# B turned between products, a bank of its own for the first modulation columns, the third scan inside a selection, and split query turns

## Time and profile before

| | us |
|---|---|
| median of three runs | 1421.62 |
| the three runs | 1420.0, 1421.62, 1423.72 |
| the profiled execution, its own time | 1424.93 |
| its span | 1422.8 |
| PE busy in it | 1379.6 (97%) |
| DVE busy in it | 800.9 (56%) |
| ACT busy in it | 351.1 (25%) |
| POOL busy in it | 261.1 (18%) |

### The profile page before, as it was taken

One profiled execution on the slowest core, in us unless ns is written; L12 is line 12 of the kernel. 1 busy time (PEld: TensorE's weight loads), 2 busy tenths in 40 slices (PEclk: granted clock), 3 DMA queues, 4 the chain that ended last, 5 costly groups with the idle time before them and its releaser, 6 DMA issues.

```text
span 1422.8 us, 16091 instructions
## 1 busy us (share of the span) xinstructions
PE 1379.6 (97%) x5860; PEld 860.6 (60%) x5860; DVE 800.9 (56%) x1915; ACT 351.1 (25%) x859; POOL 261.1 (18%) x261
## 2 busy tenths in 40 slices
PE   3999998999999999999999999999999999999999
PEld 2544555545544545555455566444578888888887
DVE  5777899538441453113555667112557676777363
ACT  4123221115300102111455567010022323230000
POOL 1167466305002386500000000000000000000000
PEclk9999998999999999999999999999999999999999
DMA  9672323542403112200301001030323131314120
GB/s 342 177 167 75 99 38 88 155 164 89 149 0 108 59 60 85 93 30 16 133 1 60 1 1 49 19 112 0 104 72 106 61 117 60 119 60 159 60 71 30
DMA packets 85769, 120.58 MB, mean 85 GB/s; under 512 B 15256, under 2 KB 43230, under 8 KB 85692
## 3 DMA queue, kind: packets, MB, share of 16 engines
q1 hardware_dynamic: 80992, 110.80, 24.5%
q10 hardware_dynamic: 2956, 5.05, 1.1%
q0 software_dynamic: 1744, 3.70, 1.0%
HBM read 111.00 MB, written 6.84 MB: 83 GB/s over the span
## 4 chain that ended last, share of the span: by engine, by line
PE 95%; DVE 3%; issue 1%; ACT 1%; DMA 0%; ACTq 0%; DVEq 0%
PE bank L776 24%; PE bank L1311 17%; PE bank L1337 9%; PE bank L788 8%; PE bank L1222 6%; PE bank L808 5%; PE bank L1063 4%; PE bank L1178 3%; PE bank L1202 3%; PE bank L838 2%; PE bank L1281 2%; PE bank L1075 2%; PE bank L1391 1%; PE bank L1031 1%; PE bank L1160 1%
## 5 line engine op out<-in xcount | busy, mean ns | idle before, releaser
L776 PE MATMUL bank<-arena 128*128 128x512 f32 (+1 forms) x800 | 343.9, 587 | 1.4 <-ACT arena L1659 1.0
L776 PEld LDWEIGHTS bank<-arena 128*128 128x128 f32 x800 | 151.4, 192 | 174.5 <-issue 169.4
L1311 PE MATMUL bank<-arena 128*128 128x256 f32 x1120 | 242.0, 379 | 0.0
L1311 PEld LDWEIGHTS bank<-arena 128*128 128x128 f32 x1120 | 212.7, 190 | 29.7 <-issue 0.8
L808 PEld LDWEIGHTS bank<-arena 128*128 128x128 f32 (+2 forms) x692 | 85.4, 147 | 69.2 <-issue 47.9
L1337 PE MATMUL bank<-arena 128*128 128x256 f32 x560 | 122.5, 380 | 0.0
L1337 PEld LDWEIGHTS bank<-arena 128*128 128x128 f32 x560 | 105.9, 190 | 16.1 <-issue 1.7
L808 PE MATMUL bank<-arena 128*128 128x128 f32 (+2 forms) x692 | 99.8, 284 | 14.7 <-DMA arena<-in_a_im 3.5
L788 PE MATMUL bank<-arena 128*128 128x512 f32 x256 | 113.2, 596 | 0.0
L1836 POOL TENSOR_TENSOR arena<-arena 128x1 f32<-128x1 f32 x8 | 4.4, 553 | 479.5 <-DVE arena L2037 479.5
L2560 DVE CUSTOM_DVE_ANT_0 arena<-bank,arena 128x128 f32<-128x128 f32 (+3 forms) x128 | 57.7, 488 | 58.9 <-PE bank L1178 58.1
(11 more groups left out here) (345 smaller groups left out, 1732.5 us busy)
## 6 DMA issues: line engine op xcount, KB each, us to landing
arena<-in_w_in SPq DMA_DIRECT2D x14, 2048.0 KB, 7.9
arena<-in_w_up SPq DMA_DIRECT2D x20, 1024.0 KB, 6.9
arena<-in_w_ada SPq DMA_DIRECT2D x8, 1024.0 KB, 13.2
arena<-in_w_down SPq DMA_DIRECT2D x8, 1024.0 KB, 7.4
arena<-in_w_ada SPq DMA_DIRECT2D x2, 2048.0 KB, 8.5
arena<-in_w_out SPq DMA_DIRECT2D x2, 2048.0 KB, 7.8
arena<-in_w_attn_br SPq DMA_DIRECT2D x2, 2048.0 KB, 8.5
arena<-in_w_o SPq DMA_DIRECT2D x2, 2048.0 KB, 7.9
```

Of the source, the lines that this page charges most:

```text
L776: mm = pe.matmul(ps[:, 0:n], act[:, k, 128 * t:128 * t + 128], w[:, k, 0:n], start=(k == 0), stop=(k == kt - 1))
L1311: mm = pe.matmul(ps, left[:, k, :], right[:, k, :], start=(first and k == 0), stop=(k == 3), skip_group_check=True)
```

## The change

Five edits. The naming of banks:

```diff
-        name_aux("ccol", "lam", "cols", "rb", "rb2", ("mod", 0), *[("x", k) for k in range(KT)], ("mod", 1),
-                 ("mod", 2), ("mod", 3), "c1", "c2", "bt0", "bt1", "cols2")
+        name_aux("ccol", "lam", "cols", "rb", "rb2")
+        name_aux(("mod", 0), banks=3)
+        name_aux(*[("x", k) for k in range(KT)], ("mod", 1), ("mod", 2), ("mod", 3), "c1", "c2", "bt0", "bt1", "cols2")
```

The product u by single k, with B's turns between its products:

```diff
+            def u_part(k, j0=0, j1=4, bt=None):
...
+                if bt is not None:
+                    pb = begin_aux(f"bt{bt}")
+                for j in range(j0, j1):
+                    ps = begin_proj(("u", j)) if k == 0 else pbank(("u", j))
+                    mm = pe.matmul(ps[:, :], w[:, k, 128 * j:128 * j + 128], hT[:, k, :],
+                                   start=(k == 0), stop=(k == KT - 1))
...
+                    if bt is not None:
+                        for m in range(4 * j, 4 * j + 4):
+                            mm = pe.transpose(pb[:, 32 * m:32 * m + 32], braw[bt][0:32, m:2048:GC], ident[0:32, 0:32])
...
-            u_step(0, 0, 3)
+            for k in range(3):
+                u_part(k)
             mod_turn(2)
-            u_step(0, 3, 4)
+            u_part(3, 0, 2)
             mod_turn(3)
+            u_part(3, 2, 4)
...
+            u_part(4)
             pe.wait_ge(b_in, 64)
...
-            u_step(1, 4, 8)
+            u_part(5, bt=0)
+            u_part(6, bt=1)
+            u_part(7)
```

The query turns of block two, and the wait behind `ypm`:

```diff
             for m in range(4):
                 turn(("qt2", m), [row2[:, t, 128 * m:128 * m + 128] for t in range(TT)])
+            one_rows("m00", 0, "m00", hT)
             pe.wait_ge(qrope_done, 2 * TT)
             for m in range(4):
                 turn(("qt2", 4 + m), [q2b[:, t, 128 * m:128 * m + 128] for t in range(TT)])
-
-            for m in range(4, 8):
-                aux_out(pe, ("qt2", m))
-            one_rows("m00", 0, "m00", hT)
             one_rows("m00", 1, "m00", hT)
...
-            for j in range(4):
-                proj_out(pe, ("ypm", j))
-
             def fill2(name):
                 key, t = name
+                if name == ("yp0", 0):
+                    for j in range(4):
+                        proj_out(pe, ("ypm", j))
```

The third scan, on DVE:

```diff
-            topk(2, TOPK // 8, True)
+            topk(2, 8)
+            scan(2)
+            topk(2, TOPK // 8 - 8, True)
             gelu_in(0)
             gelu_in(1)
-            scan(2)
             topk(3, TOPK // 8, True)
```

More of the change, by code:

```diff
@@ L825, in x_turns @@
                     turn((key, k), [src[:, t, 128 * k:128 * k + 128] for t in range(TT)])
-            def u_step(s, k0, k1):
-                pe.wait_ge(wu_in[s], 16)
-                w = slot_view(0, KT, 512)
[L831 to L835, removed]
-                    for j in range(4):
[L837 to L841, removed]
+            def u_part(k, j0=0, j1=4, bt=None):
+                pe.wait_ge(wu_in[k // 4], 16)
+                if k % 2:
+                    pe.wait_ge(hv_ready, k // 2 + 1)
+                else:
+                    pe.wait_ge(ha_ready, k // 2 + 1)
+                w = slot_view(0, KT, 512)
+                if bt is not None:
[4 more added lines that the diff above has]
+                                   start=(k == 0), stop=(k == KT - 1))
+                    if k == KT - 1:
+                        mm.then_inc(proj_done, 1)
+                    if bt is not None:
+                        for m in range(4 * j, 4 * j + 4):
+                            mm = pe.transpose(pb[:, 32 * m:32 * m + 32], braw[bt][0:32, m:2048:GC], ident[0:32, 0:32])
+                if bt is not None:
+                    mm.then_inc(aux_done, 1)
             def mod_turn(s):
```

## The result

| | before | changed |
|---|---|---|
| median, us (9 runs each) | 1422.06 | 1414.97 |
| lowest to highest | 1420.0 to 1423.72 | 1410.71 to 1418.6 |
| the profiled execution: time, span | 1424.93, 1422.8 | 1411.54, 1409.3 |
| mean granted clock in it | 0.99 | 0.996 |

The ratio is 0.9949, with a 95% interval of 0.9933 to 0.9964: 7.1 us faster, where 6.7 had been forecast (1415). A second group of six runs of the same kernel gave 1414.78, ratio 0.9944 (0.9932 to 0.9957).

A forecast was written before the change was run, and what follows sets the result against it. PE, busy in 97% of the span, was taken as the bound, with gains in its waits and slowed stretches. Block one's -0.8 and block two's -5.9 us made -6.7, so 1415 us; eight in ten from 1404 to 1419.

The forecast's parts named there:

- the wait that it forecast: Before PE's turns of q in block one: a new wait of 8 to 12 us for the norm of q.
- a clock that falls elsewhere: Sign of being wrong: PE's clock falling in places other than those forecast; no size given.
- (a): Turns of x at the start: bank 3 removes PE's 2.90 us wait and the chain behind moves whole, -2.9 us.
- (b): u's second half: with B's turns between products the clock stays full, -3.2 us.
- (c): B's turns within u: each of 8 returns to a large product may cost 0.2 us, +0.8 (0 to 1.6).
- (d): After u: DVE waits for B's copy, POOL's tables start 1.4 us later, PE waits under 1 us, made up by idle time.
- the turns between products cost what they save: Rival, chance 0.13: B's turns within u lose 3.2 us, taken in by the wait at q's turns; 1417.5 to 1420.
- The third scan, and what it meets: Block one: scan 13.2 us earlier saves PE 8.9, but POOL's tables stretch gelu_in from 4.2 to 14 us; new wait equals gain.
- the port costs little: Rival, chance 0.22: POOL's operations don't take turns with gelu_in; block one gives -10 to -13, so 1402 to 1407.
- The clock behind that wait: After the wait at q's turns: fallen clock costs 1.7 us in 16 turns and 1.3 in the z product.
- Block one, net: At ssm_out(3): all edits of block one together bring PE there 0.8 us earlier.
- Block two: Row 0 of m00 between the query turns saves 4.8 us, the moved wait behind ypm 1.1: sum -5.9.

The follow-up runs named there:

- changed_again: The changed kernel itself, unaltered, measured once more in a later group: 1414.78 us, ratio 0.9944.
- b_block: The changed kernel with B's 32 small turns in one block again, ahead of u's second half: 1409.7 us, ratio 0.9914.
- bank_only: The kernel before with only bank 3 for the first modulation columns: 1418.88 us, ratio 0.9975.
- pool_held_b_block: The changed kernel with POOL's last tables held until gelu_in is done and B's turns in one block: 1403.41 us, ratio 0.9869.
- b_early: The changed kernel with B's turns between u's products of k = 4 and 5, not 5 and 6: 1411.64 us, ratio 0.9934.
- scan_only: The kernel before with only the third scan moved inside the second selection: 1424.43 us, ratio 1.0015.
- gelu_late: The changed kernel with gelu_in(0) and gelu_in(1) moved behind 12 rounds of topk(3): 1410.41 us, ratio 0.9921.
- pool_held: The changed kernel with POOL's tables of the last quarter held until gelu_in(0) and gelu_in(1) are done: 1408.71 us, ratio 0.9910.
- block2_only: The kernel before with only block two's split query turns and the moved wait behind ypm: 1419.31 us, ratio 0.9975.
- the start alone: The kernel before with only bank 3 for the first modulation columns and B's turns between products of u: 1421.47 us, ratio 0.9992.
- no_scan: The changed kernel with the third scan back behind gelu_in: 1415.76 us, ratio 0.9955.

## Why the prediction was right, and where its terms were off

The sum (-6.7) met the result (-7.1), and the wait that it forecast is there at its place and size. That the number came so close was luck in part. The terms as the profiles measure them give more: with `changed_again`, whose run of 1415.19 us is near its median, block one is 2.1 us shorter up to y(3), block two 6.0 and its compressed scores 1.7, together some 10 us in the span, and 3 of them are the slow draw of the profile of before. One of its own signs of being wrong, a clock that falls elsewhere, shows in `changed_again`: at u's first records, and in the compressed scores (0.97).

**The start, (a).** Right, and too small, since it said only that the chain moves whole. The 2.90 us went. Besides, with no pause in the turns of x the clock came up within them: 2.0 us in the turns, 0.8 in `mod_turn(1)` and 2.4 in u's first 24 records. PE was 8.9 us early at ki, not 5.3: 2.9 + 5.2, and 0.8 from B's turns. In `changed_again` it was 6.6: there u's first 24 records took 12.10 us, with a granted clock of 0.68 and 0.89 from 32 to 40 us. Another 2.1 may be the draw of the profile of before.

**(b) and (c), B's turns.** In u's second half, with its turns, the clock stayed full, as forecast, in every profile that has them. The price of the switches was mis-sized: forecast 0 to 1.6 us. (With it u's second half took 19.8 us, 49.40 to 69.23, where 17 to 19 were forecast.) A group of one product and four turns takes 1.61 us, eight of them 12.9; in `b_block` the 32 turns take 3.67 us (49.88 to 53.55), and eight products at full clock 6.9. The switches cost 2.3 us. What they save is u's second half at a fallen clock: 3.2 us before, 3.1 in `b_block`, 2.7 in `bank_only`, 1.7 in `pool_held_b_block`. Of the forecast 3.2 - 0.8 there is 0.9 left at most, and in the last of them a loss of 0.6.

**(d), the waiting VectorE.** The mechanism was named, its size was off: forecast was a start of POOL's tables 1.4 us later than before and under 1 us of wait for PE, taken back by idle time. POOL's tables started at 70.41 us, 2.0 us earlier than before (72.41), and at 72.75 in `changed_again`; but PE came 8.9 and 6.6 us earlier. VectorE stood 7.8 us, PE waited 0.2 + 1.0 + 0.7 us, and this went on: y(3) is 1.7 to 3.6 us earlier in `b_block`. The rival "the turns between products cost what they save" held for this edit; its claim that the wait at q's turns takes it in did not: that wait is 8.7 us in `changed`, `b_block` and `b_early` alike.

**The third scan, and what it meets.** Right in every step: scan after a wait of 1.33 us (forecast 1.2), `ssm_out(2)` with no wait, `gelu_in` 13.5 us (14), the norm's end at 262.1 (264.9), PE's wait 8.7 us (10). (POOL's tables before were read as some 22 us; from 228.3 to 252.0 it is 23.7, which changes nothing.) `scan_only`, slower at 1.0015, shows that this edit alone returns more than it gains, and `gelu_late` and `pool_held`, each from its side, that it is POOL's tables under `gelu_in` that do it. The rival "the port costs little" is refuted. What it would have given is what keeping the two apart brings: the stretch from v(0) to y(3) is then 8 to 9 us shorter.

**The clock behind that wait.** Forecast 1.7 us in the turns and 1.3 in z, the middle between two rows; measured 3.67 - 1.91 = 1.8 and 7.95 - 7.03 = 0.9 in the changed kernel, 1.8 and 0.6 in `changed_again`, 1.7 and 0 in `scan_only`. The granted clock rose about 1.9 us after z had begun in the changed kernel, and with the last of the turns in `scan_only`. The Trainium skill's sentence that transposes don't release the clock ("TensorE: Matmul & The Clock Gate", "Part 4: PE-mode transpose") is not what these runs show: in the turns of x of the changed kernel the pace doubled while PE did nothing but turns (8 in 1.6 us, then 18 in 1.8), and in `scan_only` z was at full clock from its first record.

**Block one, net.** Forecast -0.8; in the profiles y(3) came 3.9 and 2.1 us earlier than in that of before. Two terms make the difference. The start stood at -5 and measured -6.6 and -4.5 at v(0). The third scan stood at +4.2 and measured +2.7 and +2.4 (177.8 and 177.5 us from v(0) to y(3), against 175.1), above all since the wait was 8.7 us and not 10.3.

**Block two.** Forecast 4.8 + 1.1; measured 4.9 + 1.1 in every kernel that has the edits. Not forecast, beyond a fall more or less: the compressed scores behind them take 57.7 to 64.4 us, by the clock. Over ten profiles with the edits their mean is 60.9, over four without 61.9. In `block2_only` the median is 3.5 us lower and not 6.0, with runs that all have a clock of 0.988 to 0.991: there the falls took a part back, as its profile (1419.51, near the median) shows.

**What stays open.** Why the clock falls more often in one kernel than in another: the parts alone (0.9992, 1.0015, 0.9975) multiply to 0.9982 and not to the whole (0.9949), that is 4.7 us less. In the marks they come nearer: the start alone brings 7.0 us at y(3) and the scan costs 2.0 from v(0) on, which makes -5.0, where the whole has -3.9 and -2.1. Of the 4 to 5 us that B's turns between products cost by the ratios the marks show 2 to 4, and of the 2 to 5 us that `no_scan` should have won nothing arrived. The profiles that were taken place the falls at the start, behind the last quarter's outputs and in the compressed scores; no run here tells why.

## What to carry to other kernels

When a wait of the busiest engine is taken away, write down by when its next supplier has to be ready, and count that supplier's chain anew with everything that now runs beside it: here a forecast gain of 8.9 us was met by a wait of 8.7, and the edit by itself cost 2 us, because POOL's tables moved under six VectorE operations with two SBUF operands. An edit that keeps PE at full clock can cost more than the clock, if what it delays is what another engine waits for; and spreading short turns between large products has a price of its own, 0.3 us for each return here (2.3 us for eight). In a kernel like this one compare stretches between marks, not only medians, and say which run of its kernel a profile is: the nine runs of the changed kernel lie 8 us apart.

## What the runs showed of the hardware

- VectorE operations with two SBUF operands and POOL operations took turns one for one: 3.10, 2.39, 2.39, 2.83 us for operations that last 0.7 alone. MAX8 and MATCH_REPLACE8, with one, kept 0.69 and 0.68 us with POOL busy.
- The clock rose from 1.2 to 2.4 GHz during an unbroken series of turns (8 in 1.6 us, then 18 in 1.8, then products at 0.44 us a record). During 8.7 us of wait it fell, and was at 0.54 on average from 262 to 268 us.
- Behind a block of 32 turns of 32x32 the clock fell in every profile that has one, but u's second half lost 3.2, 3.1, 2.7 and 1.7 us by it in four of them; with the turns in groups of four between products it stayed at 1.00.
- In the profile of before, the granted clock reads 1.00 from 38.6 us on, but u's records took 0.85 us until 43.5 and 0.43 from there: at the very start of that execution the column and the durations don't agree. In `scan_only` they do (0.52, 0.50 and 0.70 from 32 to 44 us, and 12.80 us for the same 24 records).
- The mean granted clock of a run orders the changed kernel's nine runs: 0.996 to 0.991 and 1410.7 to 1418.6 us. It doesn't order every kernel's: `scan_only` has 1421.83 us at 0.992 and 1425.19 at 0.993.
